# A block with an RWKV stage: the order of the walk's products, the start of the output projection, and the place of the bonus product

## The chip, the cores and the metric

The kernel runs on one core of one Trainium2 chip. The metric is the device time of one execution in microseconds; the median of three runs is 2652.95 us.

## The reference, cut to what matters

Two blocks of two layers each follow one another on 512 tokens of width 1024 (the second block has 256 context tokens beside them, 768 in all). The change lies in the first layer of the second block, the even mixer:

```python
def step(s, inp):                       # rwkv7_scan, one token, both directions
    r_t, w_t, k_t, v_t, kk_t, b_t = inp
    sa = einsum('bhij,bhj->bhi', s, kk_t)
    s = s * w_t - sa[..., None] * b_t + v_t[..., None] * k_t
    return s, einsum('bhij,bhj->bhi', s, r_t)
...
def finish(o, gate_r, four, gate_f):    # o: sum of both directions and their bonus terms
    o = ((o - mean) * rsqrt(var + RWKV_GN_EPS)) * lnx_g + lnx_b      # per head of 64
    yr = o * silu(gate_r)
    yf = fourier_mix(four) * silu(gate_f)
    return concatenate([yr, yf], -1) @ w_out
```

The bonus term of a head is `sum(r * k * r_k) * v`, the sum taken over the head's 64 channels.

## The kernel before, in words

Activations lie with the channel on the partition: a tile is 128 channels by 768 tokens (256 of the context, 512 latents). The RWKV part has 12 heads of 64, taken two at a time (one on each half of the partitions), so there are six pairs `p` = 0 to 5 (`RT` = 6). Tokens go in chunks of 64 (`NK` = 12 chunks), in two directions `d`. The recurrence inside a chunk is solved by a triangular inverse; the recurrence from chunk to chunk is `walk_pe` and `walk_act`.

Every engine has a program written out by hand in one order, and waits for named events of the others (`k.when`, `k.says`). Nothing is reordered. For a pair `p` TensorE's order in `rwkv_pe` is: head mean of the pair before (`head_mean_pe`), the low rank products of the next pair (`lora_pe`), that pair's input tiles (`pair_tiles_pe`: key, gate, query, value tile, each with its weights in a ring of two slabs that SyncE fills), the inverse's last combination (`combine_pe`), the walk, and the scores of the next pair (`scores_pe`). VectorE's order in `rwkv_dve` is: `head_centred_dve` of the pair before, the inverse (`inverse_head_dve`, which begins with a transpose; `decay_sums_dve` and `mix_keys_dve` of the next pair; `inverse_tail_dve`, which ends with transposes, L2539 and L2543), mixing of the next pair's queries and values, `operands_dve`, `out_added_dve` (L2697, L2700: it adds the walk's output banks), then the masks of the next pair's scores with `bonus_products_dve` between, and `bonus_dve` (L2478).

The walk, per chunk `c`, each step for both directions and both halves: the `rhs` product (L2640) needs the state of the chunk before; ScalarE copies it (L2682); `solved` (L2646) applies the chunk's inverse; ScalarE copies it (L2685); the state product (L2664) ends an accumulation whose other terms (L2651, L2654) need nothing of this chunk; ScalarE scales it into the next state (L2689). L2670 is the first part of the next `rhs`. `out_pe` (L2614, L2618, L2621) makes the output of the chunk before; nothing in the walk waits for it. It writes banks 4 to 7, the steps of the recurrence use banks 0 to 3.

`scores_pe(q)` makes for direction 0, then 1, six score groups (L2429, L2432), then three groups that turn operands to token order (L2447, L2449), which ScalarE copies (L2491) and between which it gathers masked scores for the inverse (`gather_act`, L2511, three times; the last needs the last group's mask). The bonus sum (L2029, by `wide_mm`, two products with a 64-block matrix of ones) stands at the end. `lora_act` (L2236) follows the last gather on ScalarE, and the next key tile (L2019) waits for its first result.

After the last walk: head mean, centring, squares, head variance, a logarithm and an exponential, three VectorE operations (`head_done_dve`), and then the output projection: `even_out_pe`, eight output tiles, each eight deep, in two token parts of 256 and 512 columns, two tiles in flight in banks 0 to 3. The eight depth tiles are the six pairs and two Fourier tiles. Before it, TensorE waits for all engines to end the stage:

```python
    rwkv_pe(k)
    end("rwkv")
    after(k, pe, "rwkv")
    even_out_pe(k)
```

Of the kernel before, what the change touches and what calls it, by code (L numbers as in the profile page):

```python
# [13 lines left out]
P = 128  # L14
# [1780 lines left out]
        k.mark(ACTE, st, "square", n)  # L1795


def out_dense_pe(k, st, name, rhs, parts):

    pe, ones, nb = k.nc.tensor, k.c("ones"), len(parts)  # L1800

    def hook(n, b, kk):
        if n == DT - 1 and b == nb - 1 and kk == 5:
            pe.wait_ge(*k.when(st, "squares added", 5))
            pe.wait_ge(*k.when(st, "square", 6))
            for t0, tn in parts:
                for j in (0, 1, 6):
                    pe.matmul(k.ps[:, OUT_BANK[tn], 0:tn], ones, out_squares(k, st, tn)[:, j, :], start=(j == 0), stop=False)  # L1808
    dense_pe(k, name, 4, rhs, parts, deep=4 // nb, hook=hook)
    pe.wait_ge(*k.when(st, "square", DT - 1))  # L1810
    for t0, tn in reversed(parts):
        pe.matmul(k.ps[:, OUT_BANK[tn], 0:tn], ones, out_squares(k, st, tn)[:, DT - 1, :], start=False, stop=True).then_inc(*k.says(PE, st, "sum", tn))


def out_rstd_act(k, st, parts, bank=OUT_BANK):

    a = k.nc.scalar
# [24 lines left out]
EVEN_POST, ODD_POST = ("post", "even", 1), ("post", "odd", 0)  # L1842


def even_out_pe(k):

    out_dense_pe(k, EVEN_POST, "ev_out", k.O, ALL)
    for kk in range(DT):
        pre_sum_pe(k, 1, kk)

# [560 lines left out]
def scores_pe(k, q):  # L2411
# [6 lines left out]
    for d in range(2):  # L2418
        pe.wait_ge(*k.when("operands", q, d))
        for i in range(NK // 2):  # L2420
            n = 6 * d + i
            if n >= 4:
                pe.wait_ge(*k.when("masked", q, (n - 4) // 6, (n - 4) % 6))
            for j in range(2):
                c = 2 * i + j
                at = slice(c * CK, (c + 1) * CK)
                for h in range(2):
                    rhs = k.AR[q % 2][half(h), d, c, :, :].rearrange("p a t -> p (a t)")
                    pe.matmul(k.ps[half(h), n % 4, j * 256:j * 256 + 128], k.A[half(h), d, at], rhs, start=True, stop=True)  # L2429
                for h in range(2):  # L2430
                    rhs = k.AR[q % 2][half(h), d, c, :, :].rearrange("p a t -> p (a t)")
                    mm = pe.matmul(k.ps[half(h), n % 4, j * 256 + 128:j * 256 + 256], k.F[half(h), d, at], rhs, start=True, stop=True)  # L2432
            mm.then_inc(*k.says(PE, "scores", q, d, i))
        if d == 0:
            pe.wait_ge(*(k.when("out added", q - 1) if q else k.when("mixed", "v", q)))
            for c in range(NK):
                for h in range(2):
                    mm = pe.matmul(k.ps[half(h), 6 + c // 8, (c % 8) * CK:(c % 8 + 1) * CK], val[half(h), c * CK:(c + 1) * CK], ident[half(h), :], start=True, stop=True)
            mm.then_inc(*k.says(PE, "values turned", q))
# [11 lines left out]
        if d == 0:  # L2451
# [3 lines left out]
                for h in range(2):  # L2455
                    mm = pe.matmul(k.ps[half(h), 6 + c // 8, (c % 8) * CK:(c % 8 + 1) * CK], k.r("flip64")[half(h), :], k.VT[half(h), 0, other, :], start=True, stop=True)
            mm.then_inc(*k.says(PE, "values flipped", q))
    pe.wait_ge(*k.when("values back", q))
    pe.wait_ge(*k.when("bonus products", q))
    wide_mm(k, 6, k.r("blk64"), k.KS, "bonus mm", q)  # L2460


def masks_dve(k, q, d):
# [48 lines left out]
    k.mark(ACTE, "gathered", p, n)  # L2512


def inverse_head_dve(k, p):

    v = k.nc.vector
    v.wait_ge(*k.when("gathered", p, 2))
    v.wait_ge(*k.now(DVE))
    settled(k, v.transpose(k.XN[:, 32:1024], k.GT[:]))  # L2520
    N2, T2 = (x[:].rearrange("p (b r) -> p b r", r=528) for x in (k.XN, k.XT))
    square = T2[:, :, 0:512].rearrange("p b (c i) -> p b c i", i=32)
    for i in range(1, 16):
        tmp = k.tmp[:, 0:2 * i * i].rearrange("p (b c j) -> p b c j", b=2, c=i)
        row = N2[:, :, 32 * i:33 * i].unsqueeze(2).broadcast_to([P, 2, i, i])
        settled(k, v.tensor_tensor(tmp, row, square[:, :, 0:i, 0:i], ALU.mult))
        settled(k, v.tensor_reduce(square[:, :, 0:i, i], tmp, AX.X, ALU.add))
# [94 lines left out]
    mm.then_inc(*k.says(PE, "chunk out", p, d, c))  # L2622


def walk_pe(k, p):

    pe, ident = k.nc.tensor, k.r("ident64")
    pe.wait_ge(*k.when("corner kept", p, 1))
    pe.wait_ge(*k.when("values back", p))
    pe.wait_ge(*k.when("by token", p, 5))  # L2630
# [4 lines left out]
    for c in range(NK):  # L2635
        if c:
            for d in range(2):
                pe.wait_ge(*k.when("state", p, d, c))
                for h in range(2):
                    mm = pe.matmul(k.ps[half(h), chain_bank(d, c, "rhs"), 0:CK], k.AR[p % 2][half(h), d, c, 0, :], k.SC[half(h), NK * d + c - 1, 2, :],  # L2640
                                   start=False, stop=True)
                mm.then_inc(*k.says(PE, "rhs", p, d, c))
        for d in range(2):
            pe.wait_ge(*k.when("rhs kept", p, d, c))
            for h in range(2):
# [1 line left out]
            mm.then_inc(*k.says(PE, "solved", p, d, c))  # L2647
        if c + 1 < NK:
            for d in range(2):
                for h in range(2):  # L2650
                    pe.matmul(k.ps[half(h), chain_bank(d, c, "state"), CK:2 * CK], k.TOK[half(h), NK * d + c, 0, :], k.VT[half(h), d, c, :], start=True, stop=False)  # L2651
                if c:
                    for h in range(2):
                        pe.matmul(k.ps[half(h), chain_bank(d, c, "state"), CK:2 * CK], ident[half(h), :], k.SC[half(h), NK * d + c - 1, 2, :], start=False, stop=False)  # L2654
        if c:
            for d in range(2):
                if c == 1 and p + 1 < RT:
                    pe.wait_ge(*k.when("mixed", "rv"[d], p + 1))
                out_pe(k, p, d, c - 1)
        for d in range(2):  # L2660
            if c + 1 < NK:
                pe.wait_ge(*k.when("solved kept", p, d, c))
                for h in range(2):
                    mm = pe.matmul(k.ps[half(h), chain_bank(d, c, "state"), CK:2 * CK], k.TOK[half(h), NK * d + c, 1, :], k.SC[half(h), NK * d + c, 0, :],  # L2664
                                   start=False, stop=True)
                mm.then_inc(*k.says(PE, "state mm", p, d, c + 1))
        if c + 1 < NK:
            for d in range(2):
                for h in range(2):
# [44 lines left out]
def head_centred_dve(k, p):  # L2714

    v, O = k.nc.vector, k.O[:, p, :]
    v.wait_ge(*k.when("head mean", p))
    v.scalar_tensor_tensor(O, flat_ps(k, 0, TA), -1.0 / 64, O, ALU.mult, ALU.add).then_inc(*k.says(DVE, "head centred", p))


def head_square_act(k, p):
# [28 lines left out]
def head_rstd_act(k, p):  # L2750

    a = k.nc.scalar
    a.wait_ge(*k.when("head variance", p))
    settled_act(k, a.activation(k.SQ[:], flat_ps(k, 0, TA), ACT.Ln, bias=k.c("eps", 2, 1), scale=1.0 / 64), "head variance read", p)
    a.activation(k.SQ[:], k.SQ[:], ACT.Exp, scale=-0.5).then_inc(*k.says(ACTE, "head rstd", p))


# [10 lines left out]
def rwkv_pe(k):  # L2768
# [3 lines left out]
    for p in range(RT):  # L2772
# [8 lines left out]
        walk_pe(k, p)  # L2781
        if p + 1 < RT:
            scores_pe(k, p + 1)
    head_mean_pe(k, RT - 1)
    head_variance_pe(k, RT - 1)


def rwkv_dve(k):
# [14 lines left out]
    for p in range(RT):  # L2803
        if p:
            head_centred_dve(k, p - 1)
        inverse_head_dve(k, p)
        if p + 1 < RT:
            for d in range(2):
# [622 lines left out]
def tensor_program(k):  # L3431
# [12 lines left out]
    end("pre 0")  # L3444
    rwkv_pe(k)
    end("rwkv")
    after(k, pe, "rwkv")
    even_out_pe(k)
    odd_queries_pe(k)
    odd_keys_pe(k)  # L3450
# [203 lines left out]
```

## Time and profile before

| what | us |
|---|---|
| median of three runs (2651.04 to 2653.15) | 2652.95 |
| profiled execution | 2653.14 |
| its span, first to last instruction | 2651.8 |
| first walk, first rhs to last output | 1488.0 to 1521.0 |
| last walk's end to first product of the projection | 2094.2 to 2106.95 |

Times in the rows are counted from the start of the span, in microseconds. A row of the timeline is a group of equal instructions that follow one another: start, busy time, engine, line, operation, what it writes and reads, the shape, the count, and in brackets how long the engine had been idle and what released it. PE is TensorE, DVE VectorE, ACT ScalarE, POOL GpSimd, SP SyncE. One float32 product of the source stands as two MATMUL records.

### The profile page before, as it was taken

Reading aid. Unit: us, or ns where it says so; the run is one execution under the profiler, and the core shown is the slowest. Engines: PE = TensorE matmul, PEld = TensorE weight load, DVE = VectorE, ACT = ScalarE, POOL = GpSimd, SP = SyncE. Lnnn points to the kernel's source line nnn. Section 1 sums busy time; section 2 is a strip of 40 time slices with the busy share of each in tenths; the row PEclk is TensorE's granted clock in tenths of the full one; section 3 lists DMA queues with packets and bytes.
Section 4 is the critical chain, followed back from the end, with each engine's and each line's share of the span. In section 5 each row is a group of like instructions: output and inputs, shape, how many; then the busy total and the mean of one; then the engine's idle time right before and its main releaser. Section 6 shows DMA issues by size and latency. Waiting matters only on the chain. (4 is left out here: it accounts for less than half of the span.)

```text
span 2651.8 us, 38129 instructions
## 1 busy us (share of the span) xinstructions
PE 2473.2 (93%) x16538; PEld 1705.8 (64%) x16538; DVE 1510.9 (57%) x2590; ACT 753.6 (28%) x1406; POOL 88.3 (3%) x157
## 2 busy tenths in 40 slices
PE   7997979999996999999999999999997898999997
PEld 3585548887442888844456768686776653556973
DVE  3884358777457878732267675959667113232442
ACT  1322231111013211111434454554454303200231
POOL 2000000001000000000000000000000000000000
PEclk9998989999998999999999998998988899999999
DMA  7222325555441333331030000000000112111002
GB/s 309 96 96 87 119 72 175 175 175 202 163 150 42 111 128 135 133 119 66 32 125 19 34 19 19 34 5 33 12 23 17 64 48 79 48 63 59 27 27 95
DMA packets 41063, 227.88 MB, mean 86 GB/s; under 512 B 4608, under 2 KB 4736, under 8 KB 24640
## 3 DMA queue, kind: packets, MB, share of 16 engines
q1 hardware_dynamic: 20304, 140.55, 14.6%
q0 software_dynamic: 20016, 82.79, 9.1%
q8 instruction: 130, 2.13, 0.3%
q10 hardware_dynamic: 576, 2.11, 0.2%
q14 instruction: 37, 0.30, 0.0%
HBM read 219.13 MB, written 6.29 MB: 85 GB/s over the span
## 5 line engine op out<-in xcount | busy, mean ns | idle before, releaser
L301 PE MATMUL ps<-G,ring 128*128 128x512 f32 x704 | 303.5, 592 | 0.0
L2019 PE MATMUL ps<-H,ring 128*128 128x256 f32 (+1 forms) x832 | 271.4, 487 | 7.6 <-ACT LW L2236 5.4
L652 PE MATMUL ps<-right_sums,left_sums 128*128 128x256 f32 x1056 | 244.5, 381 | 9.2 <-DVE right_sums L644 9.2
L301 PEld LDWEIGHTS ps<-G,ring 128*128 128x128 f32 x704 | 133.7, 190 | 166.6 <-issue 166.5
L2019 PEld LDWEIGHTS ps<-H,ring 128*128 128x128 f32 x832 | 157.4, 190 | 115.1 <-issue 91.6
L652 PEld LDWEIGHTS ps<-right_sums,left_sums 128*128 128x128 f32 x1056 | 201.7, 191 | 37.3 <-DVE right_sums L644 9.6
L301 PE MATMUL ps<-H,ring 128*128 128x512 f32 (+1 forms) x480 | 181.5, 535 | 0.9 <-DVE ls_tmp L2897 0.9
L652 PE MATMUL ps<-H,ring 128*128 128x256 f32 x704 | 163.7, 384 | 15.4 <-ACT H L595 15.4
L652 PEld LDWEIGHTS ps<-H,ring 128*128 128x128 f32 x704 | 134.3, 192 | 38.2 <-issue 15.5
L301 PEld LDWEIGHTS ps<-H,ring 128*128 128x128 f32 x480 | 91.1, 190 | 88.3 <-issue 84.9
L466 DVE SCALAR_TENSOR_TENSOR R<-ps,mod,XA 128x512 f32<-128x512 f32 x24 | 18.0, 750 | 204.9 <-PE ps L301 188.8
L719 ACT ACTIVATE C<-U,params_sb 128x512 f32<-128x512 f32 x44 | 35.8, 814 | 313.6 <-DVE U L746 313.6
L301 PE MATMUL ps<-O,ring 128*128 128x256 f32 (+1 forms) x256 | 85.4, 497 | 5.9 <-DVE O L2765 5.9
L2697 DVE TENSOR_TENSOR O<-O,ps 128x768 f32<-128x768 f32 x6 | 5.7, 954 | 145.9 <-PE ps L2621 145.9
L652 PE MATMUL ps<-H,left_sums 128*128 128x256 f32 x352 | 86.6, 387 | 0.0
L3030 PE MATMUL ps<-ring,H 128*128 128x256 f32 x384 | 85.9, 379 | 0.0
L652 PE MATMUL ps<-right_sums,ring 128*128 128x256 f32 x352 | 84.2, 381 | 0.0
L371 POOL DMA_DIRECT2D ada_late<-ada_rest x104 | 55.1, 530 | 752.4 <-DVE mod L351 415.1
L3030 PEld LDWEIGHTS ps<-ring,H 128*128 128x128 f32 x384 | 72.0, 190 | 12.1 <-issue 3.1
L1776 DVE TENSOR_SCALAR H<-ps,scalars 128x512 f32<-128x512 f32 (+1 forms) x24 | 15.2, 660 | 112.4 <-ACT sq_ctx L1793 76.7
L301 PEld LDWEIGHTS ps<-O,ring 128*128 128x128 f32 x256 | 50.3, 197 | 40.4 <-issue 36.4
L652 PEld LDWEIGHTS ps<-H,left_sums 128*128 128x128 f32 x352 | 67.9, 193 | 10.7 <-ACT H L595 1.4
(564 smaller groups left out, 4515.3 us busy)
## 6 DMA issues: line engine op xcount, KB each, us to landing
ada_late<-ada_rest POOLq DMA_DIRECT2D x104, 512.0 KB, 3.6
ring<-w_up SPq DMA_DIRECT2D x44, 1024.0 KB, 4.8
ring<-w_down SPq DMA_DIRECT2D x16, 1408.0 KB, 6.0
ring<-od_in SPq DMA_DIRECT2D x16, 1024.0 KB, 4.9
ring<-ev_in SPq DMA_DIRECT2D x15, 1024.0 KB, 4.8
ada_early<-ada_rest POOLq DMA_DIRECT2D x24, 512.0 KB, 4.6
ada_first_sb<-ada_first SPq DMA_DIRECT2D x8, 1024.0 KB, 16.2
ring<-ab_in SPq DMA_DIRECT2D x7, 1024.0 KB, 6.5
```

The source lines that it names most:

```text
L301: mm = pe.matmul(k.ps[:, (n % deep) * nb + b, 0:tn], wv[:, kk, a * P:(a + 1) * P], rhs[:, kk, t0:t0 + tn], start=(kk == 0), stop=(kk == kt ...
L371: g.dma_start(k.late[:, j % LATE, :], k.dram["ada_rest"][j]).then_inc(*k.lands(f"late_in{j % LATE}", "ada in", j))
L466: v.scalar_tensor_tensor(R[:, n, :], k.ps[:, bank(n), :], gate[:, n:n + 1], XA[:, n, :], ALU.mult, ALU.add)\
L652: return pe.matmul(product(k, n, j), lhsT[:, i, :], rhs[:, i, :], start=(i == 0), stop=(i == 3))
L719: a.activation(C, k.U[:, n % 2, 2:T + 2], ACT.Identity, bias=k.p(f"conv{l}", 4 * n + 3, 1), scale=k.p(f"conv{l}", 4 * n + 2, 1))\
L1776: ins = v.tensor_scalar(OUT[:, n, t0:t0 + tn], k.ps[:, banks[(n % deep) * nb + b], 0:tn], gates[b][:, n:n + 1], None, ALU.mult)
L2019: mm = pe.matmul(k.ps[:, bank + b, 0:tn], wv[:, kk, (i % 2) * P:(i % 2 + 1) * P], k.H[:, kk, t0:t0 + tn], start=(kk == 0), stop=(kk == DT ...
L2697: settled(k, v.tensor_tensor(O, O, flat_ps(k, 4, TA), ALU.add))
L3030: mm = pe.matmul(k.ps[:, 3 + 4 * (u % 2), 0:256], k.H[:, kk, t * P:(t + 1) * P], wv[:, kk, :], start=(kk == 0), stop=(kk == DT - 1))
```

## The change

1. In `walk_pe` the output product of direction 0 moves from behind the recurrence's free products to between `rhs` and `solved`; that of direction 1 moves behind the state product. The free terms of the state product are made in a helper. The waits for `mixed r` and `mixed v` of the next pair move along.
2. In `scores_pe` the bonus sum moves from the end to behind the score groups of direction 1.
3. The last pair's head mean and variance use banks 4 and 6 instead of 0. Between them, TensorE makes the products of seven of the eight depth tiles (all but that of the last pair, number 5) for the first two output tiles (`last_head_pe`); `even_out_pe` adds the eighth to these two and makes the other six as before. TensorE waits for the last pair's head alone instead of for all engines. `out_dense_pe` is written into `even_out_pe`.
4. The inverse's first transpose becomes a function of its own, called behind `head_centred_dve` and in front of `inverse_head_dve`.

```diff
+def even_out_part_pe(k, n, b, depth, start, stop):
+
+    g, (t0, tn) = n // 2, ALL[b]
+    wv = k.slab_view("ev_out", g, DT, 2 * P)
+    for kk in depth:
+        mm = k.nc.tensor.matmul(k.ps[:, 2 * (n % 2) + b, 0:tn], wv[:, kk, (n % 2) * P:(n % 2 + 1) * P], k.O[:, kk, t0:t0 + tn],
+                                start=(start and kk == depth[0]), stop=(stop and kk == depth[-1]))
+    return mm
+
+
+def last_head_pe(k):
+
+    pe, p, others = k.nc.tensor, RT - 1, (0, 1, 2, 3, 4, 6, 7)
+    pe.wait_ge(*k.when("slab", k.slab("ev_out", 0)))
+    pe.wait_ge(*k.when("head done", RT - 2))
+    pe.wait_ge(*k.when("fourier gated", 1))
+    even_out_part_pe(k, 0, 1, others, True, False)
+    pe.wait_ge(*k.when("out added", p))
+    wide_mm(k, 4, k.r("blk64"), k.O[:, p, :], "head mean", p)
+    even_out_part_pe(k, 0, 0, others, True, False)
+    pe.wait_ge(*k.when("head squares", p))
+    wide_mm(k, 6, k.r("blk64"), k.SQ, "head variance", p)
+    for b in range(2):
+        even_out_part_pe(k, 1, b, others, True, False)
+
+
 def even_out_pe(k):
 
-    out_dense_pe(k, EVEN_POST, "ev_out", k.O, ALL)
+    pe, st, ones = k.nc.tensor, EVEN_POST, k.c("ones")
+    pe.wait_ge(*k.when("head done", RT - 1))
+    for n in range(DT):
+        if n >= 2:
+            pe.wait_ge(*k.when("slab", k.slab("ev_out", n // 2)))
+            pe.wait_ge(*k.when("evac", "ev_out", 0, n - 2))
+        for b in range(2):
+            if n < 2:
+                mm = even_out_part_pe(k, n, b, (RT - 1,), False, True)
+            elif n == DT - 1 and b == 1:
+                even_out_part_pe(k, n, b, range(5), True, False)
+                pe.wait_ge(*k.when(st, "squares added", 5))
+                pe.wait_ge(*k.when(st, "square", 6))
+                for t0, tn in ALL:
+                    for j in (0, 1, 6):
+                        pe.matmul(k.ps[:, OUT_BANK[tn], 0:tn], ones, out_squares(k, st, tn)[:, j, :], start=(j == 0), stop=False)
+                mm = even_out_part_pe(k, n, b, range(5, DT), False, True)
+            else:
+                mm = even_out_part_pe(k, n, b, range(DT), True, True)
+        mm.then_inc(*k.says(PE, "mm", "ev_out", 0, n))
+        if n % 2:
+            k.mark(PE, "slab used", k.slab("ev_out", n // 2))
+    pe.wait_ge(*k.when(st, "square", DT - 1))
+    for t0, tn in reversed(ALL):
+        pe.matmul(k.ps[:, OUT_BANK[tn], 0:tn], ones, out_squares(k, st, tn)[:, DT - 1, :], start=False, stop=True).then_inc(*k.says(PE, st, "sum", tn))
     for kk in range(DT):
         pre_sum_pe(k, 1, kk)
...
             mm.then_inc(*k.says(PE, "scores", q, d, i))
+        if d == 1:
+            pe.wait_ge(*k.when("values back", q))
+            pe.wait_ge(*k.when("bonus products", q))
+            wide_mm(k, 6, k.r("blk64"), k.KS, "bonus mm", q)
         if d == 0:
...
-    pe.wait_ge(*k.when("values back", q))
-    pe.wait_ge(*k.when("bonus products", q))
-    wide_mm(k, 6, k.r("blk64"), k.KS, "bonus mm", q)
...
+def inverse_turn_dve(k, p):
 
     v = k.nc.vector
     v.wait_ge(*k.when("gathered", p, 2))
     v.wait_ge(*k.now(DVE))
     settled(k, v.transpose(k.XN[:, 32:1024], k.GT[:]))
+
+
+def inverse_head_dve(k, p):
+
+    v = k.nc.vector
     N2, T2 = (x[:].rearrange("p (b r) -> p b r", r=528) for x in (k.XN, k.XT))
...
+def walk_inputs_pe(k, p, d, c):
+
+    pe, ident = k.nc.tensor, k.r("ident64")
+    for h in range(2):
+        pe.matmul(k.ps[half(h), chain_bank(d, c, "state"), CK:2 * CK], k.TOK[half(h), NK * d + c, 0, :], k.VT[half(h), d, c, :], start=True, stop=False)
+    if c:
+        for h in range(2):
+            pe.matmul(k.ps[half(h), chain_bank(d, c, "state"), CK:2 * CK], ident[half(h), :], k.SC[half(h), NK * d + c - 1, 2, :], start=False, stop=False)
+
+
 def walk_pe(k, p):
 
-    pe, ident = k.nc.tensor, k.r("ident64")
+    pe = k.nc.tensor
     pe.wait_ge(*k.when("corner kept", p, 1))
     pe.wait_ge(*k.when("values back", p))
     pe.wait_ge(*k.when("by token", p, 5))
...
                 mm.then_inc(*k.says(PE, "rhs", p, d, c))
+            if c == 1 and p + 1 < RT:
+                pe.wait_ge(*k.when("mixed", "r", p + 1))
+            out_pe(k, p, 0, c - 1)
         for d in range(2):
             pe.wait_ge(*k.when("rhs kept", p, d, c))
             for h in range(2):
...
             mm.then_inc(*k.says(PE, "solved", p, d, c))
         if c + 1 < NK:
             for d in range(2):
-                for h in range(2):
-                    pe.matmul(k.ps[half(h), chain_bank(d, c, "state"), CK:2 * CK], k.TOK[half(h), NK * d + c, 0, :], k.VT[half(h), d, c, :], start=True, stop=False)
-                if c:
-                    for h in range(2):
-                        pe.matmul(k.ps[half(h), chain_bank(d, c, "state"), CK:2 * CK], ident[half(h), :], k.SC[half(h), NK * d + c - 1, 2, :], start=False, stop=False)
-        if c:
+                walk_inputs_pe(k, p, d, c)
             for d in range(2):
-                if c == 1 and p + 1 < RT:
-                    pe.wait_ge(*k.when("mixed", "rv"[d], p + 1))
-                out_pe(k, p, d, c - 1)
-        for d in range(2):
-            if c + 1 < NK:
                 pe.wait_ge(*k.when("solved kept", p, d, c))
                 for h in range(2):
                     mm = pe.matmul(k.ps[half(h), chain_bank(d, c, "state"), CK:2 * CK], k.TOK[half(h), NK * d + c, 1, :], k.SC[half(h), NK * d + c, 0, :],
                                    start=False, stop=True)
                 mm.then_inc(*k.says(PE, "state mm", p, d, c + 1))
+        if c:
+            if c == 1 and p + 1 < RT:
+                pe.wait_ge(*k.when("mixed", "v", p + 1))
+            out_pe(k, p, 1, c - 1)
         if c + 1 < NK:
             for d in range(2):
                 for h in range(2):
...
-    v.scalar_tensor_tensor(O, flat_ps(k, 0, TA), -1.0 / 64, O, ALU.mult, ALU.add).then_inc(*k.says(DVE, "head centred", p))
+    v.scalar_tensor_tensor(O, flat_ps(k, 4 if p == RT - 1 else 0, TA), -1.0 / 64, O, ALU.mult, ALU.add).then_inc(*k.says(DVE, "head centred", p))
...
-    settled_act(k, a.activation(k.SQ[:], flat_ps(k, 0, TA), ACT.Ln, bias=k.c("eps", 2, 1), scale=1.0 / 64), "head variance read", p)
+    settled_act(k, a.activation(k.SQ[:], flat_ps(k, 6 if p == RT - 1 else 0, TA), ACT.Ln, bias=k.c("eps", 2, 1), scale=1.0 / 64), "head variance read", p)
...
-    head_mean_pe(k, RT - 1)
-    head_variance_pe(k, RT - 1)
+    last_head_pe(k)
...
         if p:
             head_centred_dve(k, p - 1)
+        inverse_turn_dve(k, p)
         inverse_head_dve(k, p)
...
     rwkv_pe(k)
     end("rwkv")
-    after(k, pe, "rwkv")
     even_out_pe(k)
```

## Rows read from the trace of the kernel before

**Rows 1.** The page: TensorE's share of the span, and its granted clock in 40 slices.
```profile
PE 2473.2 (93%) x16538; PEld 1705.8 (64%) x16538; DVE 1510.9 (57%) x2590; ACT 753.6 (28%) x1406; POOL 88.3 (3%) x157
...
PEclk9998989999998999999999998998988899999999
```

**Rows 2.** Waits, 1400 to 2110: who waited for whom, total us, times, longest.
```profile
DVE O L2697 <- PE ps L2621: 145.9, 6, 42.3
ACT SC L2689 <- PE ps L2664: 67.3, 66, 1.7
...
PE ps L2568 <- DVE TC L2543: 20.0, 5, 12.4
...
DVE XN L2520 <- ACT GT L2511: 6.3, 6, 2.1
```

**Rows 3.** Timeline of one chunk of the first walk.
```profile
1495.54 0.54 PE L2640 MATMUL ps<-SC,AR 64*64 64x64 f32 x8
1495.92 0.42 ACT L2682 COPY PB<-ps 128x64 f32<-128x64 f32 x2 [0.23 <-PE ps L2640]
...
1496.18 0.54 PE L2646 MATMUL ps<-PB,TT 64*64 64x64 f32 x8
...
1496.56 0.42 ACT L2685 COPY SC<-ps 128x64 f32<-128x64 f32 x2 [0.23 <-PE ps L2646]
...
1497.02 0.28 PE L2614 MATMUL ps<-SC,V 64*64 64x64 f32 x4
...
1497.37 0.28 PE L2614 MATMUL ps<-SC,V 64*64 64x64 f32 x4
...
1497.72 0.40 PE L2664 MATMUL ps<-SC,TOK 64*64 64x64 f32 x8
...
1498.05 0.52 ACT L2689 ACTIVATE SC<-ps,EC 128x64 f32<-128x64 f32 x2 [1.07 <-PE ps L2664]
...
1498.42 0.54 PE L2640 MATMUL ps<-SC,AR 64*64 64x64 f32 x8
```

**Rows 4.** Timeline behind the second pair's scores.
```profile
1538.20 0.59 ACT L2491 COPY TOK<-ps 128x512 f32<-128x512 f32 x1 [2.07 <-PE ps L2449]
...
1539.95 1.56 PE L2029 MATMUL ps<-KS,rw_consts_sb 128*128 128x512 f32 x4
1541.35 1.45 PE L2029 MATMUL ps<-O,rw_consts_sb 128*128 128x512 f32 x4
...
1542.91 1.67 ACT L2511 COPY GT<-SC 32x124 f32<-32x124 f32 x4
...
1544.62 1.21 DVE L2520 STREAM_TRANSPOSE XN<-GT 128x992 f32<-128x992 f32 x1 [0.83 <-ACT GT L2511]
...
1546.86 31.23 PE L2019 MATMUL ps<-H,ring 128*128 128x256 f32 x96 [1.07 <-ACT LW L2236]
```

**Rows 5.** Timeline from the end of the last walk into the output projection.
```profile
2093.97 0.28 PE L2621 MATMUL ps<-SC 64*64 64x64 f32 x4
...
2096.01 1.56 PE L2029 MATMUL ps<-O,rw_consts_sb 128*128 128x512 f32 x4 [1.76 <-DVE O L2700]
...
2099.50 1.56 PE L2029 MATMUL ps<-SQ,rw_consts_sb 128*128 128x512 f32 x4 [1.93 <-ACT SQ L2726]
...
2106.95 18.61 PE L301 MATMUL ps<-O,ring 128*128 128x256 f32 x53 [5.89 <-DVE O L2765]
...
2130.32 0.38 ACT L1793 ACTIVATE sq_ctx<-ps 128x256 f32<-128x256 f32 x1 [9.37 <-PE ps L301]
...
2130.81 1.17 DVE L1776 TENSOR_SCALAR H<-ps,scalars 128x256 f32<-128x256 f32 x2 [9.07 <-ACT sq_ctx L1793]
2140.64 0.38 ACT L1793 ACTIVATE sq_ctx<-ps 128x256 f32<-128x256 f32 x1 [9.45 <-PE ps L301]
```

**Rows 6.** Stretches: us, busy us (x) by engine, PEclk, DMA share, GB/s.
```profile
1593.00:1610.00 17.00, 15.96 (x290) 15.45 (x292) 16.54 (x27) 9.38 (x21) 0.00 (x0) 0.50 0.14 55
...
2106.95:2120.05 13.10, 13.10 (x34) 8.13 (x35) 1.00 (x6) 0.00 (x0) 1.58 (x3) 0.81 0.72 278
```

More of the change, by code:

```diff
@@ L1795, in out_squares_act @@
         k.mark(ACTE, st, "square", n)
[L1798 to L1812, printed above, removed]
 def out_rstd_act(k, st, parts, bank=OUT_BANK):
@@ L2512, in gather_act @@
     k.mark(ACTE, "gathered", p, n)
-def inverse_head_dve(k, p):
+def inverse_turn_dve(k, p):
     v = k.nc.vector
```

## The prediction

> **What bounds the kernel now.** I read the page first. TensorE is busy for 93% of the span, at the full clock level for most of it [rows 1], so the time is close to the length of TensorE's own program. A change pays where it removes products or waits from that program, or a stretch at the lower level (1.2 instead of 2.4 GHz). The change touches the RWKV stage and the projection behind it, so the second view is the list of waits between 1400 and 2110 us [rows 2]. VectorE's 145.9 us in front of `out_added` are six long waits for the end of the walk: VectorE has nothing to do there, and the walk, which only TensorE and ScalarE share, sets the time of that stretch. ScalarE's 66 waits for the state product (one per chunk but the last, in each of the six walks) stand beside it. TensorE itself waits 20.0 us for the inverse's last transposes (L2543), five times; there VectorE's chain sets the time.
>
> **The walk's period.** The third view is the timeline of one chunk [rows 3]. From one `rhs` product (L2640, 1495.54) to the next (1498.42) are 2.88 us. A pair of products, one for each half, is issued in 0.117 us (the out block of three pairs, from one L2614 at 1497.02 to the next at 1497.37). Eighteen pairs make a chunk: rhs 2, solved 2, inputs 4, out 3 + 3, state 2, next rhs's free part 2. That is 2.10 us of the 2.88; the other 0.77 is waiting. Where it waits is what matters. After `solved` (1496.18) ScalarE's copy is made by 1496.98 (L2685), yet the state product starts only at 1497.72, since ten free pairs are queued in front of it: 0.74 us in which the recurrence waits for work that nobody needs. In the hops rhs to solved (copy L2682, 0.38 after the product, 0.21 each) and state to next rhs (L2689), TensorE is idle or nearly so.
>
> **Cost of the new walk.** I lay the same pairs in the new order, with a latency of 0.33 us from product to copy behind running work (L2664 to L2689), 0.38 out of idleness (L2640 to L2682), 0.21 a copy, 0.26 a state evacuation, 0.05 from the copy to the product that waits. Steady chunk: rhs 0 to 0.23; out of direction 0 to 0.59; solved of direction 0 at 0.60, the other must wait for its copy until 0.81, issued by 0.92; inputs to 1.39; state product 1.39 to 1.63 (its copies are there at 1.19 and 1.41); out of direction 1 to 1.98; free part to 2.21; the states are there at 2.03 and 2.30, so the next rhs starts at about 2.21. Laid out this way the old order gives 2.83 where the trace has 2.88, so I add the same 0.05: period 2.25, a gain of 0.63 for each of nine chunks (2 to 10), 5.7 us. Chunk 1 has two pairs less (no cross term). It gains 0.4 at the full level, and almost nothing where TensorE is at the lower level, since 16 pairs at twice 0.117 are already about its whole length; the lower level holds through the combine into the second chunk of some walks (1593 to 1610 in the second) [rows 6]; I take 0.35. The last chunk ends with the two last out blocks instead of one gap and then four: 0.45. Sum 6.5 per walk, **39 us** for six. Bounds: nothing below 0.52 of waiting recovered per chunk (30 us in all), nothing above the whole 0.77 (45 us). The new waits cost nothing by the rows: `mixed r` and `mixed v` of the next pair stand behind VectorE's queue, which is empty long before the walk ends [rows 2]; ScalarE's order is untouched.
>
> One rule speaks against packing more products into the gaps. The Trainium skill, "TensorE: Matmul & The Clock Gate", section "Wait — 56ns, not 53.3ns?", gives about 62 ns of sequencer time per MATMUL with hardware decode off, and 25 ns as the least distance. A pair is four MATMUL records, so by the first figure 18 pairs would need 4.5 us and no order could help; by the second 1.8. The 0.117 us for four in this trace (29 ns each) sit at the second, so the trace decides against the objection.
>
> **The bonus product.** It moves from behind the by-token groups of direction 1 to in front of them. It takes 1.40 us of TensorE (1539.95 to 1541.35) [rows 4]. TensorE's total is unchanged and its two events are long there, so it does not wait. But ScalarE's copies of these groups come 1.4 later (the first stood at 1538.20 directly behind its product), and behind them on ScalarE, without a break, stand gathers 1 and 2 (L2511), the table load and the decay sigmoid. VectorE waits for gather 2 before the inverse's transpose (L2520, six waits, 6.3 us) [rows 2, 4], and TensorE waits for the sigmoid before the next key tile (L2019, 1.07 us idle) [rows 4]. Both chains into the combine so start 1.4 later. VectorE's earlier bonus sum gains nothing: `head_centred` behind it needs the head mean, whose place in time is the same. Cost 6 x 1.38 = **+8 us**. Bounds: 0, if something I don't see already holds gather 2, to 11. The idleness before the key tile grows from 1.1 to 2.4 us; should the clock fall there, the start of a dense stretch pays up to 2.8 us, as it did at 2106.95 [rows 5, 6]. In passes 1 to 4 the 1.9 us of waiting for VectorE hide most of it; I add 1 us.
>
> **Centring and the inverse's turn.** Before, `head_centred_dve` already stands in front of `inverse_head_dve`, whose first instruction is the transpose. The split into two functions issues the same VectorE instructions in the same order. This costs and gains nothing, whatever hides it.
>
> **The output projection.** From the end of the last walk (2094.20) to the first product of `ev_out` (2106.95) are 12.75 us, with 2 x 1.3 us of mean and variance in them; and the first tile takes 13.1 us at a mean clock of 0.81 [rows 6], where the later ones come every 10.3 (2130.32 to 2140.64) [rows 5]. A tile is eight products of 512 and eight of 256 columns: 1.29 us for one of each, 0.86 and 0.43 by columns. Counted from the walk's end, the new order gives: tile 0 upper part, 7 x 0.86, to 6.0; mean (its input is ready at 1.8) to 7.3; lower part, 7 x 0.43, to 10.35; the squares are ready at 9.5, so the variance waits for TensorE and ends at 11.65; tile 1, 7 x 1.29, to 20.7. The head chain, 7.45 us from variance to first product [rows 5], is done at 17.8, hidden with 2.9 to spare. So mean and head chain run later and nobody sees it. Then 128 - 28 products remain. New end 20.7 + 82.6 - 18.1 = 85.2; old 12.75 + 82.6 + 2.8 = 98.15: 12.95 less. Against this, tile 2 needs tile 0 evacuated, which is finished only 1.3 us before, where the evacuation takes about 1.7 (L1793's start to L1776's end) [rows 5]: 0.45 lost. **-12.5 us**. Bounds: 9.7 if the clock falls in any case, 13 without the new wait. The slab of tile 0 and 1 is in long before. The later engines' waits on the end of the stage refer to the variance, not to the early products.
>
> **Sum.** 2653.14 (the profiled execution: 2651.8 of span and 1.3 around it) - 39 + 8 + 1 - 12.5 = 2610.6, and the median of the runs shown is only 0.2 below that execution. I predict **2611 us**, 1.6% faster. What a measurement of this kernel can tell from no change is 0.2%, 5 us.
>
> **Rivals.** (a) The bonus product is free, because ScalarE's chain has slack: 2602. For it: ScalarE idles 2 us before the group; against: TensorE's group ends that idleness, so it moves with it. 0.10. (b) The walk gains only half: the out block ahead of `solved` delays it by more than its issue, since a product's drain or a switch of banks adds to the hop; period 2.55: 2611 + 18 = 2629. For it: only one out block of three pairs is to fit in a wait of 0.26. 0.12. (c) The walk is bound by the copies and doesn't shorten: 2649, no change to be told. Against it is the 0.74 us between L2685's end and L2664. 0.03. (d) Slower, by the clock: the longer idleness in front of the key tile takes TensorE to the lower level, and it stays there through the tiles (44 us a pass, five passes). It decides from 17 us at the lower level a pass on (half of them lost, 8.7 x 5 = 43); with 20 a pass 2661. For it: the lower level lasted 17 us under small products [rows 6]; against it: under dense products it was over after 5 us [rows 5, 6]. 0.02. The Trainium skill, same page, section "What's actually happening", has activity release the clock; that the dense tile recovered agrees. (e) The forecast with its neighbours: 0.73.
>
> **Range.** Bounds of (e) taken together: 2598 to 2625; (b) pulls the upper end up. 2597 to 2630 leaves out less than 2 in 10. Faster 0.96, same 0.02, slower 0.02.
>
> **What would show it.** Distance of L2640's successors 2.2 to 2.3 instead of 2.88, with the out pairs on both sides of `solved`; ScalarE's wait before L2689 down from 1.07. The transpose L2520 later by 1.3 behind the last score group, in all six passes, and the wait before the key tile up to 2.4. No idleness before the projection, `head done` some 3 us before TensorE asks for it, tile 2 starting after 0.5 us of waiting. Wrong it would be if the period stays above 2.4, or if gather 2 doesn't move.

## The result, and the profile after

| kernel | median us (lowest to highest, runs) | ratio to the kernel before, 95% interval |
|---|---|---|
| before | 2652.36 (2651.04 to 2653.15, 4) | |
| changed | 2607.18 (2604.64 to 2610.07, 4) | 0.983, 0.9813 to 0.9848 |

The change makes the kernel 45 us faster; 42 were predicted (2611 from 2652.95), and the median lies inside the range. The profiled execution of the changed kernel took 2608.81 us with a span of 2607.5, against 2651.8 before: 44.3 less. In the rows a granted clock of 1.00 stands for 2.4 GHz and 0.50 for 1.2 GHz, the lower level. The timelines of both say where these lie. "Scores to combine" runs from the first score product of a pass to the first product of `combine_pe`, "walk" from its first `rhs` product to the start of its last output pair; all in us.

| pass | scores to combine: before, after | combine to walk: before, after | walk: before, after |
|---|---|---|---|
| 0 | 79.01, 82.81 | 7.54, 7.53 | 32.87, 27.01 |
| 1 | 71.91, 73.56 | 11.15, 11.12 | 34.57, 27.67 |
| 2 | 71.98, 73.59 | 11.12, 11.09 | 33.92, 26.43 |
| 3 | 71.93, 73.56 | 11.10, 11.11 | 33.54, 26.98 |
| 4 | 71.92, 73.54 | 11.14, 9.85 | 34.57, 26.43 |
| 5 | 58.75, 60.36 | 11.30, 11.30 | 33.65, 26.76 |
| sum | 425.5, 437.4: +11.9 | 63.4, 62.0: -1.4 | 203.1, 161.3: -41.8 |

The sixth term is the projection. From the walk's last output pair to ScalarE's square of the last output tile were 102.14 us (2093.97 to 2196.11) and are now 90.40 (2061.69 to 2152.09): -11.7. The four make -43.0; the remaining 1.3 lie before the first scores (1.0) and behind the projection.

The page of the changed kernel, to be read against [rows 1]: TensorE's instructions are as many as before, and its idle time has become less, from 178.6 us (2651.8 less 2473.2) to 162.3.
```profile
PE 2445.2 (94%) x16538; PEld 1688.6 (65%) x16538; DVE 1511.2 (58%) x2590; ACT 745.0 (29%) x1406; POOL 87.9 (3%) x157
...
PEclk9999889999998999999999998989999898999999
```

The waits of the changed kernel between 1400 and 2080 us, against [rows 2] (the lines are numbered anew: L2743 was L2697, L2735 was L2689, L2660 was L2621, L2706 was L2664, L2607 was L2568, L2554 was L2520, L2525 was L2491).
```profile
DVE O L2743 <- PE ps L2660: 102.7, 6, 35.4
...
ACT TOK L2525 <- PE ps L2486: 28.3, 24, 3.7
...
ACT SC L2735 <- PE ps L2706: 26.2, 66, 0.9
...
PE ps L2607 <- DVE TC L2582: 21.4, 5, 13.7
...
DVE XN L2554 <- ACT GT L2545: 17.0, 6, 6.5
```
The second row stood so in the kernel before:
```profile
ACT TOK L2491 <- PE ps L2449: 18.5, 24, 2.1
```
VectorE waits 43 us less for the end of the walks, which is the whole gain of that part, and ScalarE 41 us less for state products. The bill is in the second and the last row: ScalarE waits 28.3 us instead of 18.5 for the by-token groups, and VectorE 17.0 us instead of 6.3 for the last gather.

The timeline of one chunk of the changed kernel's first walk, against [rows 3] (L2689 is the `rhs` product, L2653 begins an output block, L2698 is `solved`, L2706 the state product):
```profile
1500.65 0.42 PE L2689 MATMUL ps<-SC,AR 64*64 64x64 f32 x8
1500.90 0.28 PE L2653 MATMUL ps<-SC,V 64*64 64x64 f32 x4
1500.98 0.34 ACT L2728 COPY PB<-ps 128x64 f32<-128x64 f32 x2 [0.30 <-PE ps L2689]
...
1501.25 0.46 PE L2698 MATMUL ps<-PB,TT 64*64 64x64 f32 x8
...
1501.63 0.35 ACT L2731 COPY SC<-ps 128x64 f32<-128x64 f32 x2 [0.30 <-PE ps L2698]
...
1502.01 0.40 PE L2706 MATMUL ps<-SC,TOK 64*64 64x64 f32 x8
1502.25 0.28 PE L2653 MATMUL ps<-SC,V 64*64 64x64 f32 x4
1502.34 0.52 ACT L2735 ACTIVATE SC<-ps,EC 128x64 f32<-128x64 f32 x2 [0.37 <-PE ps L2706]
...
1502.83 0.42 PE L2689 MATMUL ps<-SC,AR 64*64 64x64 f32 x8
```
From one `rhs` to the next are 2.18 us instead of 2.88. An output block stands in each of the two hops, and TensorE has 18 pairs of 0.117, 2.11 us, in a period of 2.18: it is busy nearly throughout, and the walk is now bound by the issue of TensorE's products; of the recurrence's waits 0.07 us a chunk are left. ScalarE's wait in front of L2735 is 0.37 us, where it was 1.07.

The timeline behind the second pair's scores in the changed kernel, against [rows 4] (L2062 is `wide_mm`, of KS the bonus, of O the head mean):
```profile
1534.05 1.56 PE L2062 MATMUL ps<-KS,rw_consts_sb 128*128 128x512 f32 x4
...
1536.73 0.58 ACT L2525 COPY TOK<-ps 128x512 f32<-128x512 f32 x1 [3.63 <-PE ps L2486]
...
1538.48 1.56 PE L2062 MATMUL ps<-O,rw_consts_sb 128*128 128x512 f32 x4
...
1541.42 1.67 ACT L2545 COPY GT<-SC 32x124 f32<-32x124 f32 x4
...
1543.12 1.21 DVE L2554 STREAM_TRANSPOSE XN<-GT 128x992 f32<-128x992 f32 x1 [2.09 <-ACT GT L2545]
```
Counted from the pass's first score product, ScalarE's first copy of a by-token group of direction 1 came at 17.23 us (1538.20 less 1520.97) and comes now at 18.86 (1536.73 less 1517.87); the inverse's transpose came at 23.65 and comes at 25.25. Both are 1.6 later. The low rank products of these passes have changed too, before and after:
```profile
1542.73 1.77 PE L2029 MATMUL ps<-WL,ws 64*128 64x512 f32 x8
```
```profile
1539.97 2.17 PE L2062 MATMUL ps<-WL,ws 64*128 64x512 f32 x5
```
Before, the products of both directions (64 rows each) ran side by side in one group of eight. Now the first runs alone, and the second (the fifth record, at 1541.45) starts when ScalarE's copy of group 5 ends (1541.39), since it writes into the bank that this copy reads. All low rank products together take 4.33 us instead of 3.06, and the wait of the key tile behind them is 1.06 us, as it was.

The timeline of the changed kernel behind its last walk, against [rows 5] (L1833 are the products of the projection in their new helper):
```profile
2061.90 6.28 PE L1833 MATMUL ps<-O,ring 128*128 128x512 f32 x14
...
2068.01 1.45 PE L2062 MATMUL ps<-O,rw_consts_sb 128*128 128x512 f32 x4
2069.30 3.19 PE L1833 MATMUL ps<-O,ring 128*128 128x256 f32 x14
...
2072.32 1.45 PE L2062 MATMUL ps<-SQ,rw_consts_sb 128*128 128x512 f32 x4
2073.61 11.77 PE L1833 MATMUL ps<-O,ring 128*128 128x256 f32 x36
...
2078.61 0.96 DVE L2811 TENSOR_TENSOR O<-O,keys 128x768 f32<-128x768 f32 x1
...
2084.22 0.38 ACT L1793 ACTIVATE sq_ctx<-ps 128x256 f32<-128x256 f32 x1 [7.35 <-PE ps L1833]
...
2086.02 14.44 PE L1833 MATMUL ps<-O,ring 128*128 128x256 f32 x49 [0.64 <-DVE H L1776]
```
TensorE has no wait from the walk to 2085.4. The head is done at 2079.6, three microseconds before its first use (2073.61 and 28 records of tile 1, 9.0 us). Then 0.64 us pass until the first tile is evacuated.

The timeline of the changed kernel at the second low rank product of pass 0, which waits for ScalarE's copy of group 5:
```profile
1424.02 0.69 PE L2062 MATMUL ps<-WL,ws 64*128 64x512 f32 x1 [1.41 <-ACT TOK L2525]
```

Stretches of the changed kernel, in the columns of [rows 6]: behind the scores before pass 0, and from the last walk on.
```profile
1424.90:1431.70 6.80, 6.80 (x17) 4.11 (x14) 5.37 (x20) 6.73 (x10) 0.54 (x1) 0.51 0.07 19
...
2061.92:2082.50 20.58, 20.58 (x66) 12.26 (x65) 6.29 (x13) 5.15 (x5) 0.38 (x1) 1.00 0.00 1
```

### The profile page after: what moved, and what is told of

The parts are those of the page before. It is cut to its first block, busy times and chain, and to the rows that moved or that the text cites. A ratio compares the mean times of both kernels' runs of the same rounds, so it can differ in the third digit from the quotient of the medians.

```text
span 2607.5 us, 38131 instructions
## 1 busy us (share of the span) xinstructions
PE 2445.2 (94%) x16538; PEld 1688.6 (65%) x16538; DVE 1511.2 (58%) x2590; ACT 745.0 (29%) x1406; POOL 87.9 (3%) x157
## 3 DMA queue, kind: packets, MB, share of 16 engines
q10 hardware_dynamic: 576, 2.11, 0.2%
## 4 chain that ended last, share of the span: by engine, by line
PE 82%; DVE 12%; ACT 4%; issue 1%; DMA 1%; SPq 0%; DVEq 0%; ACTq 0%
PE ps L652 20%; PE ps L301 18%; PE ps L2052 3%; PE ps L3076 3%; PE ps L1833 3%; PE ps L812 2%; PE ps L1484 2%; PE ps L429 2%; PE ps L3265 2%; DVE XT L2577 2%; DVE tmp L2576 2%; PE ps L2071 1%; PE ps L2462 1%; PE ps L2465 1%; PE ps L2617 1%
## 5 line engine op out<-in xcount | busy, mean ns | idle before, releaser
L1833 PE MATMUL ps<-O,ring 128*128 128x512 f32 (+1 forms) x256 | 83.6, 487 | 0.6 <-DVE H L1776 0.6
L344 DVE CUSTOM_DVE_ANT_0 ada_late<-ada_late,c_row,params_sb 128x1024 f32<-128x1024 f32 x56 | 70.0, 1281 | 7.4 <-DMA ada_late<-ada_rest 7.2
L652 PEld LDWEIGHTS ps<-right_sums,ring 128*128 128x128 f32 x352 | 67.5, 192 | 9.3
L429 PE MATMUL ps<-H,ab_first_sb 128*128 128x512 f32 x128 | 57.2, 610 | 14.4 <-ACT H L410 14.4
```

Source lines behind the costliest of these rows:

```text
L344: v.tensor_tensor_reduce(w, w, k.c_row[:], 1.0, bias, ALU.mult, ALU.add, k.MOD[part][:, tile, :])\
L429: mm = pe.matmul(k.ps[:, n, :], k.W8[:, kk, n * P:(n + 1) * P], k.H[:, kk, 0:T], start=(kk == 0), stop=(kk == DT - 1))
L652: return pe.matmul(product(k, n, j), lhsT[:, i, :], rhs[:, i, :], start=(i == 0), stop=(i == 3))
L1833: mm = k.nc.tensor.matmul(k.ps[:, 2 * (n % 2) + b, 0:tn], wv[:, kk, (n % 2) * P:(n % 2 + 1) * P], k.O[:, kk, t0:t0 + tn], start=(start and ...
```

## The experiments

Ten kernels ran, each beside the kernel before.

| label | median us | ratio, 95% interval |
|---|---|---|
| e1_walk | 2613.06 | 0.9849, 0.9832 to 0.9865 |
| e2_out | 2639.38 | 0.995, 0.9936 to 0.9965 |
| e3_bonus | 2666.71 | 1.005, 1.0035 to 1.0065 |
| e4_nobonus | 2598.69 | 0.9797, 0.9782 to 0.9811 |
| e5_turn | 2651.21 | 0.9998, 0.9989 to 1.0008 |
| e6_late | 2630.63 | 0.9921, 0.9906 to 0.9936 |
| e7_gather | 2598.39 | 0.9796, 0.9781 to 0.981 |
| e8_gather_bonus | 2596.71 | 0.9795, 0.978 to 0.9809 |
| e9_one_tile | 2615.07 | 0.9857, 0.984 to 0.9873 |
| e10_turn_first | 2611.84 | 0.9852, 0.9836 to 0.9869 |

### Each part alone

**e1_walk.** `walk_pe` and its helper from the change, all else as before.

> The kernel before with the walk's new order alone. If the terms of the prediction add up (theory A), each steady chunk goes from 2.88 to 2.18 us and the time falls by 40 to 42 us, to about 2611, and the stretch from the scores to the combine keeps its 71.9 us in passes 1 to 4. If the shorter walk only pays together with the other edits (theory B, the clock or the early bonus product help it), it gains under 35.

Measured: 2613.06, 39 us less. The six walks take 160.8 us, 42.3 less, at the same 2.18 a chunk, and the stretches before the combine keep their 71.9. So the walk stands by itself. Three of the 42.3 are not in the total. Two of them are found behind the last walk, 104.1 us from its last pair to ScalarE's last square where the kernel before has 102.1: the lower clock level comes earlier there and takes in the last pair's head mean and variance, 2.71 and 2.93 us where [rows 5] has 1.56 each. The first tile of the projection isn't slower for it (12.6 us, where it was 13.1).
```profile
2054.32 2.71 PE L2029 MATMUL ps<-O,rw_consts_sb 128*128 128x512 f32 x4 [1.76 <-DVE O L2707]
...
2058.96 2.93 PE L2029 MATMUL ps<-SQ,rw_consts_sb 128*128 128x512 f32 x4 [1.92 <-ACT SQ L2733]
```

**e2_out.** `last_head_pe`, `even_out_part_pe` and `even_out_pe` with the two banks, all else as before.

> The kernel before with the early start of the output projection alone. Theory A: 12.5 us less, to about 2640, of which 2.8 are the first tile's time at the lower clock level and 9.7 idleness filled. Theory B (the lower level comes anyway, since the head chain's vector and scalar work still stands between): 10 us less or under.

Measured: 2639.38, 12.5 less; the span behind the last walk is 12.0 us shorter. Theory A. The granted clock is 1.00 throughout the beginning, as in the changed kernel.

**e3_bonus.** Only this:
```diff
+        if d == 1:
+            pe.wait_ge(*k.when("values back", q))
+            pe.wait_ge(*k.when("bonus products", q))
+            wide_mm(k, 6, k.r("blk64"), k.KS, "bonus mm", q)
...
-    pe.wait_ge(*k.when("values back", q))
-    pe.wait_ge(*k.when("bonus products", q))
-    wide_mm(k, 6, k.r("blk64"), k.KS, "bonus mm", q)
```

> The kernel before with the bonus product in front of the by-token groups alone. Theory A: slower, by 1.4 to 1.6 us in each of six passes plus some 2 us for a lower clock level in the first pass, together 10 to 12, to about 2663. Theory B: ScalarE's and VectorE's chains have room and it costs nothing, 2652.

Measured: 2666.71, 14.9 us slower by the medians and 13 by the ratio, somewhat more than expected. Scores to combine: 82.81, then 73.55 on average in passes 1 to 4, 60.36; the sum is 11.9 us more, the same as in the changed kernel. The walks give another 1.2, nearly all in pass 0 (34.01 instead of 32.87), where the second chunk takes 3.80 us instead of 2.64. Theory A, and this part of the change is a loss.

**e4_nobonus.** The changed kernel with that diff undone.

> The changed kernel with the bonus product back at the end of the scores. Theory A: 10 to 12 us faster than the changed kernel, 2595 to 2597, the stretch from scores to combine back to 71.9 us in passes 1 to 4 and about 79 in the first. Theory B: no difference to be measured, 2607.

Measured: 2598.69, 8.5 less than the changed kernel by the medians; by the spans of the profiled executions 10.8 (2596.7 and 2607.5). Scores to combine is back at 79.00, 71.96, 71.97, 71.96, 71.92 and 58.74. Theory A; by the median the gain is a little under the 10 to 12 that were expected, by the spans inside.

**e5_turn.** The kernel before with the inverse's turn in a function of its own.
```diff
         if p:
             head_centred_dve(k, p - 1)
+        inverse_turn_dve(k, p)
         inverse_head_dve(k, p)
```

> The kernel before with the inverse's turn as a function of its own, as in the change: the same instructions in the same order on every engine. Theory A: the time of the kernel before within 2 us, 2652. Theory B (some of the gain hides in this edit): under 2647.

Measured: 2651.21, ratio 0.9998. VectorE's instructions stand in one and the same order in the kernel before, this one and the changed one; so do ScalarE's. The whole change acts through TensorE's program: its order, its waits and the banks that it writes.

### What bounds the walk

**e6_late.** The changed kernel with both output blocks behind the state product:
```diff
-            if c == 1 and p + 1 < RT:
-                pe.wait_ge(*k.when("mixed", "r", p + 1))
-            out_pe(k, p, 0, c - 1)
...
         if c:
-            if c == 1 and p + 1 < RT:
-                pe.wait_ge(*k.when("mixed", "v", p + 1))
-            out_pe(k, p, 1, c - 1)
+            for d in range(2):
+                if c == 1 and p + 1 < RT:
+                    pe.wait_ge(*k.when("mixed", "rv"[d], p + 1))
+                out_pe(k, p, d, c - 1)
```

> The changed kernel with both output products of a chunk behind the state product, none in the wait between rhs and solved. Theory A (both waits of a chunk can hold three pairs and no more; the pairs of the prediction's layout): six pairs and the free part behind the state product are 0.3 us longer than that hop, and the first wait stays empty; period 2.5 to 2.6 us instead of 2.18, some 3.9 us a walk, 23 in all, about 2630. Theory B (all the gain came from freeing the state product): period 2.2, 2607.

Measured: 2630.63, with a period of 2.51 us. Its timeline:
```profile
1500.57 0.40 PE L2689 MATMUL ps<-SC,AR 64*64 64x64 f32 x8
...
1501.16 0.45 PE L2695 MATMUL ps<-PB,TT 64*64 64x64 f32 x8 [0.20 <-ACT PB L2726]
```
The `rhs` product waits no more for the state but for the free products in front of it, while TensorE stands idle in the hop from `rhs` to `solved`. Of the 0.70 us that the new order wins, freeing the state product gives 0.37 (2.88 to 2.51), and filling the first hop 0.33. Theory A.

### Why the bonus product costs

**e7_gather.** e4_nobonus with ScalarE's second gather moved:
```diff
         if g == 2:
...
             gather_act(k, q, 0)
-        elif g == 4:
             gather_act(k, q, 1)
```

> The changed kernel with the bonus product back at the end, and ScalarE's gather 1 directly behind gather 0, in front of the copies of groups 3 and 4, where ScalarE was idle for 2 us. Theory A (ScalarE's chain sets the inverse's start and the key tile's): from scores to combine 0.8 us less in passes 1 to 5, where head_centred is next to hold the transpose, and about 1 less in pass 0; 5 us in all, about 2594. Theory B (it is hidden): 2599, as with the gather in its old place.

Measured: 2598.39, the time of e4_nobonus. The transpose stands at 23.53 us behind the scores, where it was at 23.67, in passes 1 to 5, and scores to combine gains 0.1 us there. In pass 0, where no head mean stands in between, it gains 1.6 (77.39). Theory A's number failed: the wait of ScalarE is used, but the gather now makes ScalarE's copy of group 3 late, TensorE waits for it before group 5, and with group 5 the head mean and the centring move, which hold the transpose next. The timeline of e7_gather shows this wait:
```profile
1529.06 0.33 PE L2480 MATMUL ps<-rw_consts_sb,F 64*64 64x64 f32 x4 [0.39 <-ACT TOK L2524]
```

**e8_gather_bonus.** The same edit in the changed kernel, with the early bonus product.

> The changed kernel, early bonus product and all, with gather 1 moved forward in the same way. Theory A (the early bonus product costs what it does only because gather 1 stands behind the copies that it delays): its price is gone, about 2594 to 2597, and the wait of 1.4 us before the second low rank product in pass 0 with it. Theory B (the product costs by its place in TensorE's own order): 8 us or more slower than the same kernel with the bonus product at the end, 2602 or more.

Measured: 2596.71, 10.5 less than the changed kernel, and no difference to be told from e4_nobonus and e7_gather. Scores to combine is 71.5 in passes 1 to 4 where the changed kernel has 73.6, and 78.4 in pass 0 where it has 82.8; the wait before the second low rank product of pass 0 is gone. Against e7_gather, with the same gathers and the late bonus product, that is 1.0 more in pass 0 and 0.3 less in each of the others: nothing in sum. In its timeline the transpose begins without a wait behind the centring, and the key tile waits 0.24 us:
```profile
1536.11 0.96 DVE L2763 SCALAR_TENSOR_TENSOR O<-ps,O 128x768 f32<-128x768 f32 x1 [3.48 <-PE ps L2062]
...
1537.17 1.21 DVE L2553 STREAM_TRANSPOSE XN<-GT 128x992 f32<-128x992 f32 x1
...
1539.19 9.30 PE L2052 MATMUL ps<-H,ring 128*128 128x256 f32 x29 [0.24 <-ACT LW L2269]
```
The bonus product's place in TensorE's order costs nothing in sum as soon as the gather is not queued behind what it delays: theory A.

**e10_turn_first.** The changed kernel with the two calls exchanged:
```diff
-        if p:
-            head_centred_dve(k, p - 1)
         inverse_turn_dve(k, p)
+        if p:
+            head_centred_dve(k, p - 1)
```

> The changed kernel with head_centred behind the inverse's turn instead of in front of it. Theory A (the order centring, turn is worth its place, since centring fills VectorE's wait for gather 2): the 0.96 us of centring come into VectorE's chain in passes 1 to 5, 4.8 us slower than the changed kernel, about 2612. Theory B (VectorE's chain has room there): 2607.

Measured: 2611.84, 4.7 more. Scores to combine grows by 1.2 in passes 1, 2 and 4, by 2.8 in pass 3 and 0.8 in pass 5, and in passes 1 to 3 the combine behind is shorter by 1.2, 1.5 and 3.0 us (9.93, 9.60 and 8.15). Over the three stretches of all passes that is 3.2 us more, by the spans of the profiled executions 2.7. So the order that the change names is worth some 3 to 5 us, a difference that the intervals of the two ratios don't separate; the kernel before had it already. The time is that of theory A, but its path, VectorE's chain, holds for pass 5 alone, where the combine still waits for VectorE. In passes 1 to 4 the last transposes come only 0.85 us later, and the combine starts without a wait for them, where TensorE waited 1.9 us in the changed kernel. TensorE itself is late: its fourth low rank product waits for the centring, since both use one bank.
```profile
1544.93 1.55 PE L2062 MATMUL ps<-AL,ws 64*128 64x512 f32 x4 [2.36 <-DVE O L2764]
```

### How much of the projection is hidden

**e9_one_tile.** The changed kernel with the seven-depth products of the second tile left where they were, behind the last head:
```diff
-    for b in range(2):
-        even_out_part_pe(k, 1, b, others, True, False)
...
-            if n < 2:
+            if n < 1:
```

> The changed kernel with only the first output tile begun before the last head is done; the second is made whole behind it. Theory A: 9.03 us of products are taken from a wait in which TensorE then stands idle for 6.2 us: 6 us slower than the changed kernel, and up to 3 more if the clock falls in it, 2613 to 2616. Theory B (the head chain is delayed as much by the first tile as it gains from it, the second hides nothing): 2607.

Measured: 2615.07, 7.9 more. Its timeline has the wait that the second tile filled:
```profile
2080.45 10.10 PE L1833 MATMUL ps<-O,ring 128*128 128x256 f32 x27 [5.85 <-DVE O L2809]
```
Theory A. From the walk's last pair to ScalarE's last square are 97.7 us instead of 90.4. Of the 9.0 us of products taken out, 5.85 come back as waiting; the other 3 had bought nothing, since the head was done 3.0 us before its use. The rest of the 7.3 goes with the granted clock, 0.50 from 2078.0 to 2084.6, which the changed kernel doesn't have here. So the head chain is a wait of fixed length, and what is put into it is won until it is full.

## Why the prediction was right, point by point

**The walk: right, 39 foreseen, 41.8 measured** in the timelines. The period was put at 2.25 and is 2.18. The layout gave 2.21; the 0.05 added on top, because the old order came out 0.05 short in the same layout, was not there. Nine chunks of 0.07 in six passes are 3.8 us; the third chunk, which takes 2.29, gives 0.7 of it back. The last chunk gained 0.43 (0.45 foreseen), the second chunk 0.34 on average (0.35 foreseen), but with 1.5 gained in pass 4 and 0.8 lost in pass 0. The measured 0.70 a chunk lies inside the bounds of 0.52 and 0.77, and the period of 2.18 speaks against rivals (b) and (c); e6_late shows both hops to count (2.5 to 2.6 foreseen there, 2.51 measured). The rule that was weighed, 62 or 25 ns a MATMUL in the Trainium skill ("TensorE: Matmul & The Clock Gate", "Wait — 56ns, not 53.3ns?"): 72 records in 2.18 us are 30 ns each, so the trace stays with the second.

**The bonus product: right in sign and in the chain through ScalarE, 8 + 1 foreseen, 11.9 measured, and 1.2 in the walk of pass 0.** Three sizes were off. The price per pass was taken as the product's 1.40 us and is 1.6. The 0.2 more are not settled by an experiment. A change between products of 64 and of 128 rows stands on either side of the product now, where before it stood beside another of 128 rows; 0.1 us passes between the last score product's slot and 1534.05. The Trainium skill, "TensorEngine Tiling (Array Packing)", "Key Properties", says that a change of tiling mode drains the array; that the row shows such a gap agrees, and no run here takes the change of mode alone. Second, pass 0 pays 3.8 instead of 1.6. TensorE has no wait in front of the combine of this pass, before or after, so its own program sets the time there. No head mean stands between the by-token groups and the low rank products. The second of these waits for ScalarE's copy of group 5, 1.41 us, and the clock is at the lower level from 1424.9 to 1431.7, over the other low rank products and the start of the next key tile. Third, the walk of pass 0 pays too: its second chunk is at the lower level and takes 3.46 us, where e1_walk and e4_nobonus, with the same walk, have 2.18. All five kernels with the early bonus product and the gather in its old place (the changed one, e3, e6, e9, e10) have the lower level at both places of pass 0; the five with the late product and that gather (the one before, e1, e2, e4, e5) have it at neither. By e3_bonus the whole price is 11.9 + 1.2 = 13.1 us.

The prediction named that the clock might fall, but placed the wait wrongly, and this sign of its list did not come: it expected 2.4 us in front of the key tile, where passes 1 to 4 still have 1.06 and pass 0 has none. The key tile is 1.6 us later in passes 1 to 4, as ScalarE's chain has it, but the low rank products in front of it last 1.3 us longer and fill the time, for the second of them waits for the copy of group 5. Rival (a) fell by e3_bonus and e4_nobonus, rival (d) did not come. e8_gather_bonus adds what the prediction did not ask: it had gather 1 on the path, and moving that gather takes the whole price away.

**Centring and turn: right, nothing.** e5_turn.

**The projection: right, 12.5 foreseen, 11.7 measured.** The head chain is done 3.0 us before its use (2.9 foreseen), the evacuation of the first tile costs 0.64 (0.45 foreseen), and the clock level stays up.

**The sum.** -39 + 9 - 12.5 = -42.5 foreseen, -41.8 + 11.9 - 11.7 and -2.7 elsewhere = -44.3 in the profiled executions. The walk's error (2.8 too little gain) and the bonus's error (2.9 too little loss) nearly cancel; that the total was met more closely than its parts is luck.

**The parts alone don't quite add up.** By the ratios e1, e2 and e3 give -40, -13 and +13, -40 together, where the change gives -45; each has an interval of about 4 us, so that is no contradiction. In the timelines the terms do add up, but for the stretches at the lower clock level, which fall where they fall: the second chunk of a walk takes 2.3 to 3.5 us in one and the same program, the combine of pass 4 9.85 us in the changed kernel where it was 11.14, and the stretch behind the last walk 2.0 more in e1_walk.

The fastest kernels of this study are e4_nobonus, e7_gather and e8_gather_bonus, 2597 to 2599, some 2.0% under the kernel before.

## What to carry to other kernels

In a chain that goes to and fro between two engines, work that nobody waits for belongs into the hops, split so that each piece is no longer than its hop: lay out one period on paper with the measured latencies, and count the queued pieces in front of each product that the chain needs. When a product is moved forward, ask not only whether its inputs are there, but what it pushes back, and follow that through the other engines' queues: 1.4 us on TensorE in front of a copy cost 1.6 in two engines' chains, and the cure was to move an instruction of a third. Where two parts of one change pull in different directions, the total hides it: each part wants its own run.

## What the runs showed of the hardware

Two things were not expected. A 128-row product put between 64-row products delays what follows by 1.6 us, where it takes 1.40 with another of 128 rows behind it. And the places of the lower clock level shift between kernels whose programs are the same up to there. The rows show it for the kernel before and for e5_turn, which has its instructions in its order. In pass 1 the combine starts at 1592.88 in the one and at 1591.86 in the other; the lower level is there at once in the first and 7 us later in the second.
```profile
1592.90:1598.70 5.80, 5.80 (x112) 5.80 (x114) 5.66 (x10) 5.21 (x7) 0.00 (x0) 0.52 0.38 157
```
```profile
1591.90:1598.70 6.80, 4.86 (x162) 4.77 (x163) 6.62 (x12) 5.38 (x7) 0.00 (x0) 1.00 0.33 134
```
From this combine to the walk are 11.15 us in the kernel before and 9.51 in e5_turn, and the walk's second chunk takes 3.81 and 3.08. The changed kernel and e9_one_tile, alike up to the last walk, have 3.45 and 2.32 us in the second chunk of pass 1. A difference of 2 to 3 us between two kernels here can be that alone, and ten executions of e5_turn lie between 2647.88 and 2657.09 us. What falls in the same place in every kernel with the same edit, as in pass 0 behind the early bonus product, is not of this kind.
